# Three edits at the seams of a two-block transformer on one core: early first rows, the square root's table, and the order of scores and turns

## The reference, cut to what matters

```
# layer 0
h = rms_norm(x, norm_g);  qa, ka, va, qb, kb, vb, qi, ki, wi, gate = split(h @ w_in)
for each block of 128 queries:
  p_m = softmax(qa_m @ ka_m.T * scale + bias, chunk mask)    m = 0, 1;  4 heads
  o_a = (p_0 - lam * p_1) @ va;   o_a = rms_norm(o_a) * const
  o_b = softmax(qb @ kb.T * scale + bias, mask, top 256 keys) @ vb   8 heads
x1 = x + (concat(o_a, o_b) * silu(gate)) @ w_o
# layer 1
h = rms_norm(x1, norm_g);  q_lat, kv_lat, k_rope, gate = split(h @ w_in)
... 16 heads of attention, x2' = x1 + (o * silu(gate)) @ w_o
x2 = rms_norm(x2', final_norm)
# the second block
h = rms_norm(x2, norm_mix_g) * (1 + sc1) + sh1;  u_f, q, k, v = split(h @ w_in)
... Fourier mix, window attention, experts
```

## Time and profile before

| | us |
|---|---|
| three runs | 2674.8, 2676.23, 2676.85 |
| median | 2676.23 |
| profiled execution | 2675.31 |
| its span (first to last instruction) | 2673.5 |
| busy in the span: PE, DVE, ACT, POOL | 2488.0, 1724.0, 1253.4, 514.2 |
| mean granted TensorE clock | 0.963 of full |

### The profile page before, as it was taken

One profiled execution on the slowest core, in us unless ns is written; L12 is line 12 of the kernel. 1 busy time (PEld: TensorE's weight loads), 2 busy tenths in 40 slices (PEclk: granted clock), 3 DMA queues, 4 the chain that ended last, 5 costly groups with the idle time before them and its releaser, 6 DMA issues. The chain is left out here.

```text
span 2673.5 us, 32112 instructions
## 1 busy us (share of the span) xinstructions
PE 2488.0 (93%) x11653; PEld 1615.7 (60%) x11653; DVE 1724.0 (64%) x3272; ACT 1253.4 (47%) x2023; POOL 514.2 (19%) x513
## 2 busy tenths in 40 slices
PE   7999999799999799989999996999994799999998
PEld 3344444355555687446556666985552588888886
DVE  2799999767765421325654546515565588888886
ACT  2221111244554256445455543244444477777774
POOL 0000001101101000007776660000123111111111
PEclk9999999799999899999999998998997799999999
DMA  3011841201100414045343224030014799999995
GB/s 134 8 63 34 74 98 38 98 28 45 36 29 28 144 56 108 12 125 168 119 127 108 84 81 150 4 127 32 32 48 173 288 379 385 384 386 391 389 386 195
DMA packets 131130, 374.19 MB, mean 140 GB/s; under 512 B 22568, under 2 KB 39672, under 8 KB 129440
## 3 DMA queue, kind: packets, MB, share of 16 engines
q1 hardware_dynamic: 114512, 316.53, 32.2%
q0 software_dynamic: 16464, 55.61, 9.4%
HBM read 327.00 MB, written 45.11 MB: 139 GB/s over the span
## 5 line engine op out<-in xcount | busy, mean ns | idle before, releaser
L513 PE MATMUL ps<-l_hT,l_w 128*128 128x512 f32 (+1 forms) x832 | 364.1, 596 | 2.6 <-DVE l_hT L242 2.6
L513 PEld LDWEIGHTS ps<-l_hT,l_w 128*128 128x128 f32 (+1 forms) x832 | 155.2, 189 | 204.2 <-issue 204.1
L973 ACT ACTIVATE a_pT<-ps 128x512 f32<-128x512 f32 (+3 forms) x368 | 164.0, 486 | 159.4 <-PE ps L857 158.6
L901 PE MATMUL ps<-l_wo,a_mixT 128*128 128x512 f32 x384 | 181.5, 600 | 3.4 <-ACT l_klT L997 1.1
L1546 DVE MAX8 l_best<-sel 128x8 f32<-128x384 f32 (+5 forms) x192 | 171.6, 893 | 5.4
L985 ACT ACTIVATE a_p<-ps,a_stat 128x384 f32<-128x384 f32 (+7 forms) x192 | 129.1, 673 | 89.6 <-DVE a_stat L1059 52.4
L1547 DVE MATCH_REPLACE8 sel<-l_best,sel 128x384 f32<-128x384 f32 (+5 forms) x192 | 168.1, 876 | 0.0
L985 ACT ACTIVATE l_lat<-ps,a_stat 128x1024 f32<-128x1024 f32 (+7 forms) x128 | 94.7, 740 | 150.0 <-DVE a_stat L1059 149.1
L842 PE MATMUL ps<-l_kT,l_raw 96*128 96x512 f32 (+3 forms) x384 | 147.3, 492 | 5.7 <-ACT l_lat L985 4.1
L857 PE MATMUL ps<-ident,a_p 128*128 128x128 f32 x608 | 99.3, 292 | 32.1 <-DVE a_p L1072 28.6
L2783 POOL DMA_INDIRECT out_dram<-m_q,e_token x15 | 34.0, 2267 | 452.3 <-DVE m_q L2981 452.3
(11 more groups left out here) (488 smaller groups left out, 5763.2 us busy)
## 6 DMA issues: line engine op xcount, KB each, us to landing
x_raw<-in_w_gate SPq DMA_DIRECT2D x25, 2048.0 KB, 11.2
x_raw<-in_w_down SPq DMA_DIRECT2D x24, 2048.0 KB, 10.3
x_raw<-in_w_up SPq DMA_DIRECT2D x23, 2048.0 KB, 11.6
ada_w<-in_w_ada POOLq DMA_DIRECT2D x64, 384.0 KB, 3.7
m_ufT<-in_w_up SPq DMA_DIRECT2D x9, 2048.0 KB, 12.0
m_ufT<-in_w_down SPq DMA_DIRECT2D x8, 2048.0 KB, 12.9
l_w<-in_e_w_in SPq DMA_DIRECT2D x7, 2048.0 KB, 8.6
m_ufT<-in_w_gate SPq DMA_DIRECT2D x7, 2048.0 KB, 10.0
```

Of the source, the lines that this page charges most:

```text
L513: last = nc.tensor.matmul(self.t.ps[0:m, bank, :], w[:, c, col * P:col * P + m], hT[:, c, half * 512:(half + 1) * 512], start=c == 0, stop ...
L901: last = nc.tensor.matmul(t.ps[:, 7, :], self.lhs_out(n, self.order[n], c), self.w_out[:, c, h * 512:(h + 1) * 512], start=c == 0, stop=c ...
L973: self.k.nc.scalar.activation(dst, src, ACT.Copy).then_inc(self.moved["act"], 1)
```

## The change

There are three edits.

1. **First rows.** The row block with which the projections of layer 1 and of the mix begin is loaded by SP at the end of the attention before, into a buffer that outlives the stage (`early_rows`). `SummedNorm.load` returns at once for row 0. DVE scales row 0 alone (`dve_scale_first`); rows 1 to 7 are scaled on ACT (`act_scale`, a copy with a factor per partition). The order on ACT at the start becomes: high part of the first weight half, high part of row 0, scale of row 1, high part of the second weight half, scale of row 2. On DVE the low part of a weight half comes ahead of the row's low part for rows 0 and 1, and the second strip's two halves are split over rows 5 and 6.
2. **The table.** `PairAttention.act` of a0 and a1 runs one small square root (with its table load) ahead of the last two half squares.
3. **Scores ahead of turns**, in a0 only (`if self.heads`): the scores of a step are issued before both turns.

```
@@ SummedNorm
     def load(self, e, b):
         n = len(self.xbuf)
+        if b == 0:
+            return
         if b >= n:
             e.wait_ge(self.turned, (b - n + 1) * self.NG)
         e.dma_start(self.X(b), self.src[b * P:(b + 1) * P, :]).then_inc(self.x_in[b % n], 16)
-    def dve_scale(self, e, b):
+    def dve_scale_first(self, e):
+        e.wait_ge(self.early, 16)
+        self.nc.vector.tensor_scalar(self.X(0), self.X(0), self.stat[:, 1, 0:1], None, ALU.mult).then_inc(self.scaled, 1)
+
+    def act_scale(self, e, b):
         n = len(self.xbuf)
-        e.wait_ge(self.x_in[b % n], 16 * (b // n + 1))
-        self.nc.vector.tensor_scalar(self.X(b), self.X(b), self.stat[:, 1, b:b + 1], None, ALU.mult).then_inc(self.scaled, 1)
+        e.wait_ge(self.x_in[b % n], 16 * (b // n + (b % n > 0)))
+        self.nc.scalar.activation(self.X(b), self.X(b), ACT.Copy, scale=self.stat[:, 1, b:b + 1]).then_inc(self.scaled, 1)
@@ SplitProjection
         norm.dve_roots(e)
-        norm.dve_scale(e, 0)
-        norm.dve_scale(e, 1)
+        norm.dve_scale_first(e)
         for b in range(NB):
             norm.dve_move(e, b)
-            if b == 1:
-                self.dve_low_half(e, 0, 1)
+            if b < 2:
+                self.dve_low_half(e, 0, b)
             norm.dve_low(e, b)
-            if b == 0:
-                self.dve_low_half(e, 0, 0)
-            if b == 5:
-                self.dve_low(e, 1)
-            if b + 2 < NB:
-                norm.dve_scale(e, b + 2)
+            if b in (5, 6):
+                self.dve_low_half(e, 1, b - 5)
     def act_item(self, e, item):
-        if len(item) == 1:
+        if item == (0,):
+            self.act_high_half(e, 0, 0)
+            self.norm.act_high(e, 0)
+            self.norm.act_scale(e, 1)
+            self.act_high_half(e, 0, 1)
+            self.norm.act_scale(e, 2)
+        elif len(item) == 1:
             self.norm.act_high(e, item[0])
+            if item[0] + 2 < NB:
+                self.norm.act_scale(e, item[0] + 2)
@@ PairAttention.pe
+            if self.heads:
+                self.pe_scores(e, *second, *first)
             if groups:
                 self.pe_turn(e, cur, 0)
-            self.pe_scores(e, *(second + first if self.tiled else second))
+            if not self.heads:
+                self.pe_scores(e, *(second + first if self.tiled else second))
             if groups > 1:
                 self.pe_turn(e, cur, 1)
@@ PairAttention.act
+            self.k.nc.scalar.activation(self.warm[:], self.t.ident[:, 0:1], ACT.Sqrt)
             for half in range(2):
                 self.sums.act_half(e, self, half)
@@ layer0_attend, SP
+            e.wait_ge(at.y_stored[0], 16)
+            e.dma_start(early_rows, t.x1_d[order[0] * P:(order[0] + 1) * P, :]).then_inc(early, 16)
             at.store_end(e, t.x1_d)
@@ layer1_attend, SP
+            e.wait_ge(at.scored_by[1], at.per * (NB - 1))
+            e.wait_ge(at.y_stored[order.index(0) % 2], 16 * (order.index(0) // 2 + 1))
+            e.dma_start(early_rows, t.x2_d[0:P, :]).then_inc(early, 16)
             load_x(NB - 1)
```

More of the change, by code:

```diff
@@ L263, with __init__ @@
     BANKS, NG = 4, 2
-    def __init__(self, k, tag, t, src, gain, split, whole, xbuf, last, mod=None, twice=False):
+    def __init__(self, k, tag, t, src, gain, split, whole, xbuf, last, early, mod=None, twice=False):
+        self.early = early
         self.nc, self.t, self.src, self.gain, self.split, self.whole = k.nc, t, src, gain, split, whole
@@ L578, in act_high, with act_high_half @@
         for half in range(2):
-            e.wait_ge(self.raw_in[half], 16 * (i + 1))
-            self.k.nc.scalar.activation(self.w[slot][:, half * KD // 2:(half + 1) * KD // 2, 0:n], self.raw[half][:, :, 0:n],
-                                        ACT.Copy).then_inc(self.highs, 1)
+            self.act_high_half(e, i, half)
+    def act_high_half(self, e, i, half):
+        n, slot = self.strips[i].n, self.slot[i]
+        e.wait_ge(self.raw_in[half], 16 * (i + 1))
+        self.k.nc.scalar.activation(self.w[slot][:, half * KD // 2:(half + 1) * KD // 2, 0:n], self.raw[half][:, :, 0:n],
+                                    ACT.Copy).then_inc(self.highs, 1)
     def dve_low(self, e, i):
@@ L1349 @@
 SEL_LEN = _at
+EARLY0, EARLY1 = 1664, 776
 def layer0(k, a, t):
@@ L1720, in layer1_project @@
     nl = Q_LORA + KV_LORA + C_ROPE
-    xbuf = [k.sb(f"n1_x{i}", [P, D])[:] for i in range(3)]
+    xbuf = [k.sb(f"n1_x{i}", [P, D])[:] for i in (1, 2)]
     whole = [k.sb(f"n1_whole{i}", [P, KD, P])[:] for i in range(2)]
-    norm = SummedNorm(k, "n1", t, t.x1_d, a["o_norm_col"], hT, whole, xbuf, before.order[NB - 1])
+    norm = SummedNorm(k, "n1", t, t.x1_d, a["o_norm_col"], hT, whole, [before.early_rows, *xbuf], before.order[NB - 1], before.early)
     flat = [x.rearrange("p c n -> p (c n)") for x in norm.whole]
@@ L1733, in layer1_project @@
         Strip("T", 512, [(0, W[:, nl + 512:nl + 1024])], gate.put(1)),
-    ], (512, 512), raw, range(4, 8), norm, {(0,): 0, (4,): 1, (1, 3): G0, (G0, 1): G1})
+    ], (512, 512), raw, range(4, 8), norm, {(4,): 1, (1, 3): G0, (G0, 1): G1})
+    k.sb("n1_x0", [P, D])
     with ExitStack() as s:
@@ L2212, in mixing_project @@
                       [ufT[:, i, :].rearrange("p (c n) -> p c n", n=P) for i in (1, 2)],
-                      [*(qT[:, i, :] for i in range(4)), *(kk[:, i, :] for i in range(2))], before.order[NB - 1],
+                      [before.early_rows, *(qT[:, i, :] for i in (0, 1, 3)), *(kk[:, i, :] for i in range(2))], before.order[NB - 1], before.early,
                       (t.mod[:, KD:2 * KD], t.mod[:, 0:KD]), twice=True)
@@ L2229, in mixing_project @@
         Strip("T", 512, [(0, W[:, 0:512])], put_T(nc, ufT)),
-    ], (512, 384), raw, range(4, 8), norm, {(0,): Q, (4,): QKV, (QKV, 1): U},
+    ], (512, 384), raw, range(4, 8), norm, {(4,): QKV, (QKV, 1): U},
         [(i, j) for i in (Q, QKV) for j in range(NB)] + by_pair)
```

6 lines of the change are left out of this document (added).

## The result

The changed kernel takes 2643.59 us (median of four runs, 2642.26 to 2645.08); the kernel before took 2675.52 (four runs) on the same chip. The ratio is 0.988, with a 95% interval of 0.9864 to 0.9896. The sign was right and so were the mechanisms in the main; what a0 nets and when the first weight half lands were not.

A forecast was written before the change was run, and what follows sets the result against it. PE was taken to bound most of a0. Gains of 9.2 (a0), 3.5 (layer 1's start) and 8.0 (mixing projection), 20.7 us from 2675.31, gave 2654.6, predicted as a median of 2655.5; range 2648 to 2667.

The forecast's parts named there:

- Net of a0: 20.6 − 11.4 = 9.2: Scores ahead of turns in a0: 20.6 of 28.6 us of subtraction waits go, 11.4 of new losses come; bounds 2 and 13.
- the landing of the first weight half: Layer 1's and the mix's starts: without row 0's 512 KB ahead, landing at 886.7 instead of 888.1, 1616.8 instead of 1618.2.
- the exponential's loop of 6.0: Wide joined steps of a0: scores, maximum, exponential take 6.0 us, under PE's 6.13 of work, so PE stays the bound.
- The bubbles: Unjoined wide pairs of a0: second turn waits for ACT's copies of the first, 0.45 us each, 15 times, 6.8 together.
- the squares: a0: a square on ACT between exponential and copies, no longer covered by scores, three times some 0.45, 1.4 us.
- rival 1: a0: waits only move, bubbles of 0.9 us make 20 us of losses, a0 gives nothing, 2664.7 us; chance 0.22.
- 3.2 us of bubbles: a0: loss of 1.5 us in block 0's unjoined pairs and about as much in narrow ones, 3.2 in all.
- the 1.1 counted for it: Mixing projection, second strip: clock needn't fall behind a wait of 2.7 us, 1.7 gained less 0.6 for the chance it does.
- rival 2: a0: brief idle moments in wide pairs drop TensorE's clock to 0.50, up to 40 us lost, 2695; chance 0.04.
- The table: Square root's table loaded ahead of the last squares in a1 and a0: costed at 0, up to 1.3 us if wrong.
- its best case, 13 us for a0: Upper bound of a0's gain, with bubbles hidden behind ACT's idle time.

The follow-up runs named there:

- e9: e6 with scores ahead of turns only in a0 pairs that are joined or at most 512 wide, other pairs in the old order: 2628.25 us, ratio 0.9826.
- e4: Kernel before, order kept, but joined pairs turn the first map once both exponentials are there, the second map's share left out of the result: 2653.49 us.
- e3: Changed kernel with 512 KB of row 0 transferred once more, unread, ahead of the first weight half in both projections: 2648.14 us, ratio 0.9897.
- e6: Changed kernel with both low parts of the second strip made on DVE behind row 7, not behind rows 5 and 6: 2636.01 us, ratio 0.9849.
- e7: Changed kernel with edit 2 undone, the square root's table loaded at the start of the projections again: 2644.51 us, ratio 0.9885.

## Why the prediction was wrong

What failed first is the term "Net of a0: 20.6 − 11.4 = 9.2", which measured 16.4: the 20.6 took each wait at its reported idle time, and 3.2 of the 11.4 were losses that did not come. The second is the landing of the first weight half, taken 1.4 us earlier and measured 2.7 and 3.6 earlier. To see which part of a0 it was, its 64 pairs are sorted by kind; each step runs from one pair's result on DVE to the next, and the sum over a kind is compared.

| kind of step, number | before | after | e9 | change | forecast |
|---|---|---|---|---|---|
| wide joined, with the first of a block, 16 | 107.29 | 94.54 | 93.13 | −12.8 | −13.4 |
| wide not joined, 16 | 111.22 | 120.14 | 110.37 | +8.9 | +8.2 |
| narrow joined, with the first, 12 | 52.14 | 44.53 | 44.53 | −7.6 | −4.9 |
| narrow not joined, 12 | 56.96 | 55.83 | 55.84 | −1.1 | +1.7 |
| block 0, all of it | | | | −3.8 | −0.8 |

(The last row is the rest of the 16.4. A wide pair is one over 512.)

**Wide joined pairs: right.** PE's work of 6.13 us was said to be over the exponential's loop of 6.0. Block 6's step fell from 6.98 to 6.01 and its last one from 7.31 to 6.36, so it is the loop or something close to it that binds, by a tenth; e4 has the same two steps in the old order. That the sum came so near is partly luck: block 7 gave 3.0 where I had 4.2 (some 0.5 more stands in block 0's row, where the wait for its first pair begins), blocks 4 to 6 gave 9.8 where I had 9.2.

**The bubbles: right in mechanism, and in size as a sum.** I took 0.45 for each of 15 pairs and 1.4 for the squares, 8.2 together; measured are 8.9, of which the waits on the copies report 4.7. They are not spread as I had it: the first such pair of a block lost 1.0 to 1.4, the last 0.4 or nothing, and in the first stands the longer wait for the exponential (0.7 instead of 0.3). What the squares cost was not separated. e9 gives these pairs their old order back and 9.8 us with it, so all of it is a pure loss. The forecast's higher bound, 0.9 each, did not come, so rival 1 is out.

**Narrow joined pairs: the term mis-sized.** What goes was read off the reported idle time, 4.9. The steps lost 7.6. e4 takes the wait away without touching the order, and the twelve steps lose 6.8: 1.9 us more than was reported, 0.16 each. Idle time in a trace runs from the modelled end of a product to the next start, and without a wait the next one starts 0.17 before that end, as the rows at e4 show. The clock is no rival here: it was at full in all of blocks 1 to 6, before and after.

**Narrow pairs that aren't joined, and block 0: charged for losses that did not come.** I moved 3.2 us of bubbles into them by analogy with the wide pairs. But a narrow pair has one turn, and its scores still lie between it and the one before: there is nothing to wait for, and the steps became 0.1 shorter each, by the one place fewer at which a load starts together with its product (in e4, in the old order, they didn't). In block 0 the waits on the subtraction fell from 6.4 to 0.9, where I had let 2.3 go; 1.7 in front of the sum, on the copies, and 1.5 on the exponential stand there now, and 3.8 are gained net instead of 0.8. The clock has little part in it: in the changed kernel it came up at 526.5 for 3.4 us inside this block, and before only at 539.0, but e3 and e6, with the same a0 and at half the clock in all of the block, are 3.4 us shorter there too. How the 3.4 splits further was not tested.

**The starts: mis-sized landing.** The 1.4 us by which the weight half was to land earlier were 2.7 and 3.6 (of which 0.4 is the earlier issue). I spread the 512 KB of row 0 over all that is under way; e3 shows how far what is issued ahead delays what stands behind: putting it back makes 4.3 us to landing 6.6 again in layer 1, and 4.5 in the mix 7.1. The links on ACT, with the scale that no row showed, were right to 0.1 each. The turn in front of the first product took 0.4 less than I had in layer 1; in the mix the chain took 6.0 us for 5.6, since the high part of row 0 waited for DVE's move. Behind the first product of layer 1 there was one more microsecond: the clock came up 3.3 us behind it instead of 5.5.

**Behind the mix's first product: the clock.** The rows follow one another at 5.11 us, near the 5.04 forecast, and the two waits are 3.1 and not 3.9. But I expected the clock to stay up behind the longer one, and it fell behind 2.13 for 3.4 us, a loss of 1.7 as before: the 1.1 counted for it didn't come. That makes 3.0 − 1.1 + 0.8 = 2.7 for 1.8 measured, and 0.9 is less than this stretch varies between kernels of the same code (3.9).

**The clock in a0 (rival 2)** stayed at 1.00 through 20 bubbles. The Trainium skill, "TensorE: Matmul & The Clock Gate", section "A second HAM failure mode: psum-queue depth-cycling", tells of a kernel whose clock swings because TensorE idles briefly and often between groups that cycle through accumulator banks. The row from 560 to 855 disagrees for bubbles of this size.

**The table** was costed at nothing; e7 says 0.0 in layer 1 and 0.9 in the mix. I had followed the chain in the first and not in the second.

The range failed because its ends were built from the same reported waits as its middle: its best case, 13 us for a0, hid some of the losses but left the waits at their reported size, and 16.4 is beyond it by 3.4. Layer 1 passed its upper bound too, 6.3 for 5.5. The mix, 8.8, lay within its own.

## What to carry to other kernels

Reorder an in-order engine only where it waits: the same edit won 20 us at pairs with a dependence in front and lost 9 at pairs without one, and leaving those out (e9) was worth more than any repair. A reported wait on TensorE at full clock is worth its idle time and another 0.2 here, since the row of the product before it ends later than the next could have started, so sum periods between marks, not idle columns. Of several transfers issued together, put the one that is waited for first: 512 KB ahead of it moved its landing by 2.3 and 2.6 us.

## What the runs showed of the hardware that I had not expected

A wait's hidden price on TensorE, about 0.2 us: in e4 blocks 1 to 6 became 3.8 us shorter than the waits that went report, and 0.17 of a single wait can be seen (600.76 against 598.34). A weight load for operands of 64 rows behind one for 128, or the other way, starts together with its product and not ahead of it (601.12, 601.76, 600.18), also where nothing is waited for. The bubbles of 0.25 us between the two turns of a wide pair never lowered the granted clock, and it fell behind one wait of 2.13 us, for 3.4 us.
